# Hybrid decoder step on one core: expert queries and scores head by head, gathers behind the first query tile, and the lead of the first table at 20

## The reference

```
a  = RMSNorm(x);  p = a @ w_in            # GLA heads q,k,v,gate + MoBA heads q,k,v
o  = [gated linear attention | block attention over a paged cache]
h  = x + o @ w_out
c  = RMSNorm(h)
q  = c @ w_peer_q                         # 8 heads x 2 halves x 64
s1, s2 = q[half 0] @ sub_keys, q[half 1] @ sub_keys      # 128 keys per half
16 best of each half -> 256 sums -> 16 best: 16 experts of 16384 per token and head
g  = softmax(their scores)
hid = gelu(c . u_tab[expert]);   h += sum over heads and experts of g * hid * v_tab[expert]
h += sigmoid(h @ w_ple_gate) * (p @ w_ple_proj);  y = RMSNorm(h)
```

## Time and profile before

| | us |
|---|---|
| median of 3 runs | 2666.64 |
| profiled execution | 2673.36 |
| its span | 2671.8 |
| PE busy | 2126.1 (80%) |
| DVE busy | 1123.9 (42%) |
| POOL busy | 696.2 (26%) |
| ScalarE busy | 371.6 (14%) |

### The profile page before, as it was taken

How to read it: one execution, slowest core, us unless ns; L and a number is a source line. 1 busy time by engine, 2 the same in 40 slices (tenths; PEclk the granted TensorE clock), 3 DMA queues, 4 the chain that set the end, 5 groups by cost and what they waited for, 6 DMA issues and landing times.

```text
span 2671.8 us, 27603 instructions
## 1 busy us (share of the span) xinstructions
PE 2126.1 (80%) x9678; PEld 1228.2 (46%) x9678; DVE 1123.9 (42%) x2202; ACT 371.6 (14%) x780; POOL 696.2 (26%) x598
## 2 busy tenths in 40 slices
PE   8997899899798899467777777777777777776797
PEld 5775565555576677322222222223222222223466
DVE  2000001100185211677667667666555555445312
ACT  2000110001343000211111111111111101101111
POOL 0000000000000000464454454444444444444210
PEclk9998999999866899689999999999999998998898
DMA  4347999996421332599999999999999999999971
GB/s 158 140 163 281 364 344 367 343 355 264 168 74 45 130 141 83 229 415 422 421 421 421 422 421 421 421 421 422 421 421 422 421 421 418 421 421 421 376 287 68
DMA packets 139859, 854.80 MB, mean 320 GB/s; under 512 B 16385, under 2 KB 17218, under 8 KB 54258
## 3 DMA queue, kind: packets, MB, share of 16 engines
q0 software_dynamic: 85248, 612.41, 55.4%
q1 hardware_dynamic: 53938, 238.80, 23.5%
q10 hardware_dynamic: 576, 2.36, 0.2%
HBM read 844.07 MB, written 9.44 MB: 319 GB/s over the span
## 4 chain that ended last, share of the span: by engine, by line
DMA 43%; PE 42%; DVE 5%; issue 4%; SPq 3%; ACT 2%; POOL 1%; POOLq 0%; DVEq 0%; ACTq 0%
DMA big<-in_vt,big 32%; PE ps L736 14%; PE ps L1072 7%; PE ps L829 6%; DMA aT<-in_vt,big 5%; DMA big<-in_u,big 4%; PE ps L1097 3%; PE ps L782 2%; PE ps L845 2%; DMA subk<-in_v 1%; DVE big L1437 1%; SPq L344 1%; PE ps L1088 1%; SPq L336 1%; DMA wring<-in_u,big 1%
## 5 line engine op out<-in xcount | busy, mean ns | idle before, releaser
L1072 PE MATMUL ps<-big,wring 128*128 128x512 f32 x1232 | 583.0, 618 | 253.6 <-DMA big<-in_vt,big 206.1
L1437 DVE CUSTOM_DVE_ANT_0 big<-big 128x2048 f32<-128x2048 f32 x206 | 472.4, 2293 | 351.9 <-DMA big<-in_u,big 342.6
L1072 PEld LDWEIGHTS ps<-big,wring 128*128 128x128 f32 x1232 | 228.6, 195 | 605.9 <-issue 429.8
L1072 PE MATMUL ps<-aT,wring 128*128 128x512 f32 x816 | 375.4, 603 | 124.7 <-DMA aT<-in_vt,big 124.6
L484 POOL DMA_INDIRECT big<-in_vt,big x174 | 210.5, 1210 | 441.7 <-PE ps L1072 350.6
L476 POOL DMA_INDIRECT big<-in_u,big x206 | 238.6, 1158 | 330.3 <-DVE big L1419 254.8
L1072 PEld LDWEIGHTS ps<-aT,wring 128*128 128x128 f32 x816 | 147.7, 190 | 352.0 <-issue 228.4
L736 PE MATMUL ps<-aT,wring 128*128 128x288 f32 x1024 | 251.7, 409 | 3.2 <-DVE aT L1147 3.2
L1437 DVE CUSTOM_DVE_ANT_0 big<-wring,big 128x2048 f32<-128x2048 f32 x82 | 188.0, 2293 | 137.9 <-DMA wring<-in_u,big 134.2
L736 PEld LDWEIGHTS ps<-aT,wring 128*128 128x128 f32 x1024 | 196.2, 192 | 58.6 <-issue 4.0
L829 PE MATMUL ps<-aT,wring 128*128 128x288 f32 x768 | 207.2, 425 | 1.4 <-ACT big L543 1.4
(11 more groups left out here) (297 smaller groups left out, 1822.6 us busy)
## 6 DMA issues: line engine op xcount, KB each, us to landing
big<-in_kT SPq DMA_DIRECT2D x128, 512.0 KB, 6.2
wring<-in_w_in SPq DMA_DIRECT2D x48, 1024.0 KB, 5.1
big<-in_v SPq DMA_DIRECT2D x48, 512.0 KB, 6.5
wring<-in_v SPq DMA_DIRECT2D x32, 512.0 KB, 5.0
states<-in_v SPq DMA_DIRECT2D x32, 512.0 KB, 5.6
wring<-in_w_out SPq DMA_DIRECT2D x16, 1024.0 KB, 4.8
big<-in_w_ple SPq DMA_DIRECT2D x9, 1024.0 KB, 9.0
subk<-in_v SPq DMA_DIRECT2D x16, 512.0 KB, 6.8
```

The lines of the kernel that those rows point to most:

```text
L1072: mm = pe.matmul(ps[:, 4 * t + c, :], diag[:, j % 4, :], vring2[j % VR][:, c * 512:(c + 1) * 512], start=(j % P == 0), stop=(j % P == P - ...
L1437: dve.tensor_tensor_reduce(prod, uring[j % UR], cnat[:, tile_of(j), :], 1.0, 0.0, ALU.mult, ALU.add, hid[:, j:j + 1]).then_inc(u_read, 1)
```

## The change

1. PE works head by head: query tile 0, the scores of head 0 for both prompt groups, the transposes of prompt group 0, then query tiles 1 to 7, with the scores of head h-1 behind tile h from h = 2 on; then the scores of head 7, the transposes of group 1, and the sample scores and transposes.
2. The sample tokens are no longer repeated by DVE. PE writes them to the four quarters of the partitions, 64 matmuls of 32 columns for the scores and 64 for the transposes.
3. Query weights use two slots of `wring` only; the scores lie where the other two were. u's ring is seven slots of `big`, v's is one of `big`, two of `wring` and two of `aT`.
4. POOL issues the first u row when DVE has the first table. Its waits stand inside the loop: for the eighth query tile ahead of v 1, for the last transposes ahead of v 3.
5. LAG is 20 instead of 16.
6. ScalarE copies queries and scores head by head, with the first exponentials behind query 3 and the first GELU behind query 6. DVE waits for the scores of each next head by itself. DVE's sixteen memsets of `iota16` move ahead of the output projection.

The diff, cut to its core:

```diff
-LAG = 16
+LAG = 20
...
-        slot = [big[:, (3 + k) * D:(4 + k) * D] for k in range(8)]
-        o = 11 * D
+        slot = [big[:, 2 * D + PH * N + k * D:2 * D + PH * N + (k + 1) * D] for k in range(8)]
+        o = 10 * D + PH * N
...
-        uring = slot[0:5] + [wflat[:, (2 + k) * D:(3 + k) * D] for k in range(2)]
-        vring2 = slot[5:8] + [flata[:, k * D:(k + 1) * D] for k in range(2)]
+        scores01 = wflat[:, 2 * WS:2 * WS + 32 * P].rearrange("p (a t s k) -> p a t s k", t=2, s=2, k=P)
+        scores2 = st[:, 0:16 * P].rearrange("p (s a k) -> p s a k", s=2, k=P)
...
-            with sp.Fori(0, NPQ // SLOTS) as i:
-                weights(i, WT, A["w_pq"], W_PQ)
+            for h in range(NPQ):
+                if h < 2:
+                    sp.wait_ge(w_slots_free, NMO + NOUT + h + 1)
+                else:
+                    sp.wait_ge(query_mm, h - 1)
+                sp.dma_start(wring[:, h % 2, 0:WT], A["w_pq"][h, :, :]).then_inc(w_in[h % 2], 16)
...
-            pool.wait_ge(score_mm, 12)
-            pool.wait_ge(cn_mm, 12)
             for j in range(NU):
+                if j == 1:
+                    pool.wait_ge(query_mm, NPQ)
+                if j == 3:
+                    pool.wait_ge(cn_mm, 12)
...
+            def query_copied(h):
+                act.wait_ge(query_mm, h + 1)
+                act.activation(qpT[:, h, :], ps[:, h % 2, 0:N], ACT.Copy).then_inc(query_out, 1)
+
+            def scores_copied(h):
+                act.wait_ge(score_mm, h + 1)
+                for hf in range(2):
+                    act.activation(scores01[:, h, :, hf, :], ps[:, 2 + 2 * (h % 2) + hf, 0:2 * P].rearrange("p (t k) -> p t k", k=P),
+                                   ACT.Copy).then_inc(score_out, 1)
...
+            query_copied(0)
+            scores_copied(0)
+            turned(0)
+            for h in range(1, NPQ):
+                query_copied(h)
+                if h >= 2:
+                    scores_copied(h - 1)
+                if h == 3:
+                    exponentials(0)
+                if h == 6:
+                    gelu(0)
+            scores_copied(NPQ - 1)
+            turned(1)
+            act.wait_ge(states_gone, 1)
+            for q in range(4):
+                act.wait_ge(score_mm, PH + q + 1)
+                act.activation(scores2[:, q // 2, 4 * (q % 2):4 * (q % 2) + 4].rearrange("p a k -> p (a k)"), ps[:, q, :], ACT.Copy).then_inc(score_out, 1)
+            turned(2)
...
-                if turn_ % 2 == 0 and turn_ < 2 * heads:
+                if turn_ % 2 == 0 and 0 < turn_ < 2 * heads:
...
+            def query_tile(h):
+                pe.wait_ge(w_in[h % 2], (NMO + NOUT) // SLOTS * 16 + (h // 2 + 1) * 16)
+                if h >= 2:
+                    pe.wait_ge(query_out, h - 1)
+                for kt in range(KT):
+                    if h == 0:
+                        pe.wait_ge(normed, KT + kt + 1)
+                    mm = pe.matmul(ps[:, h % 2, 0:N], wring[:, h % 2, kt * P:(kt + 1) * P], aT[:, kt, :], start=(kt == 0), stop=(kt == KT - 1))
+                mm.then_inc(query_mm, 1)
+
+            def head_scores(h):
+                pe.wait_ge(query_out, h + 1)
+                if h == 1:
+                    pe.wait_ge(cn_out, 4)
+                if h >= 2:
+                    pe.wait_ge(score_out, 2 * h - 2)
+                for t in range(2):
+                    for hf in range(2):
+                        rows = slice(64 * hf, 64 * hf + 64)
+                        mm = pe.matmul(ps[:, 2 + 2 * (h % 2) + hf, t * P:(t + 1) * P], qpT[rows, h, t * P:(t + 1) * P],
+                                       subk[rows, h, :], start=True, stop=True)
+                mm.then_inc(score_mm, 1)
+
+            def sample_scores():
+                pe.wait_ge(score_out, 2 * PH)
...
+                        for c in range(4):
+                            mm = pe.matmul(ps[c * TS:(c + 1) * TS, q, f * P:(f + 1) * P], qpT[rows, h, T:N], subk[rows, h, :],
+                                           start=True, stop=True, tile_position=(64 * hf, c * TS), skip_group_check=True)
...
+            def turn_normed(t):
+                lo, n = TT[t]
                 for q in range(4):
-                    if t:
+                    if t == 1 and q < 2:
+                        pe.wait_ge(score_out, 2 * PH)
+                    if t == 2:
                         pe.wait_ge(cn_out, 4 * (t - 1) + q + 1)
                     for f in range(4):
                         kt = 4 * q + f
-                        src = aT[:, kt, lo:lo + n] if t < 2 else crep[:, kt, :, :].rearrange("p g n -> p (g n)")
-                        mm = pe.transpose(ps[:, 4 + q, f * P:(f + 1) * P], src, ident[:, :])
+                        if t < 2:
+                            mm = pe.transpose(ps[:, 4 + q, f * P:(f + 1) * P], aT[:, kt, lo:lo + n], ident[:, :])
+                        else:
+                            for c in range(4):
+                                mm = pe.matmul(ps[c * TS:(c + 1) * TS, 4 + q, f * P:(f + 1) * P], aT[:, kt, T:N], ident[:, :],
+                                               start=True, stop=True, tile_position=(0, c * TS), skip_group_check=True)
                     mm.then_inc(cn_mm, 1)
 
-
-
-            pe.wait_ge(score_out, 12)
+            pe.wait_ge(subk_in, 16)
+            query_tile(0)
+            head_scores(0)
+            turn_normed(0)
+            for h in range(1, NPQ):
+                query_tile(h)
+                if h >= 2:
+                    head_scores(h - 1)
+            head_scores(NPQ - 1)
+            turn_normed(1)
+            sample_scores()
+            turn_normed(2)
+            pe.wait_ge(score_out, 2 * PH + 4)
...
-            dve.wait_ge(score_out, 3)
+            dve.wait_ge(score_out, 2)
             top_head(0)
-            dve.wait_ge(normed, 2 * KT)
-            dve.wait_ge(banks_free, SLOTS + NMO + NOUT + NPQ)
-            dve.wait_ge(states_gone, 1)
-            for g in range(4):
-                dve.tensor_copy(qrep[:, :, g, :], qpT[:, :, T:N]).then_inc(rep_done, 1)
-                dve.tensor_copy(crep[:, :, g, :], aT[:, :, T:N]).then_inc(rep_done, 1)
             dve.wait_ge(cn_out, 4)
 
             for i in range(heads):
...
                 dots(j0, j0 + 4)
                 if i:
                     coefficients(2 * i - 1)
-                if i == 1:
-                    dve.wait_ge(score_out, 12)
+                if i + 1 < PH:
+                    dve.wait_ge(score_out, 2 * i + 4)
                 if i + 1 < heads:
                     top_head(i + 1)
                 weights_of(i)
                 dots(j0 + 4, j0 + 12)
                 coefficients(2 * i)
                 if 1 <= i <= PH:
+                    dve.wait_ge(score_out, 2 * PH + 4)
                     top_head(heads + i - 1)
```

More of the change, by code:

```diff
@@ L219, in program @@
         sqt = st[:, 0:N]
+        assert 2 * D + 512 <= 2 * WS
         pleT = masks[:, :, :].rearrange("p m t -> p (m t)")[:, 0:PLE // P * N].rearrange("p (k n) -> p k n", n=N)
-        pnat = [wflat[:, 0:D], st[:, 0:D]]
-        wple = ([wflat[:, D:2 * D], wflat[:, 0:D], st[:, 0:D]] + [uring[(NU - UR + i) % UR] for i in range(UR)] +
+        late0, late1 = (wflat[:, 2 * WS + k * D:2 * WS + (k + 1) * D] for k in range(2))
+        pnat = [late1, st[:, 0:D]]
+        wple = ([late0, late1, st[:, 0:D]] + [uring[(NU - UR + i) % UR] for i in range(UR)] +
                 [cnat[:, 2, :]] + [vring2[(NU - VR + i) % VR] for i in range(VR)])
@@ L617, in _, with turned @@
             root(2)
-            with act.Fori(0, NPQ // SLOTS) as i:
-                copy_out(i, W_PQ, qpT)
-            for t in range(3):
-                if t == 2:
-                    act.wait_ge(states_gone, 1)
-                for q in range(4):
-                    act.wait_ge(score_mm, 4 * t + q + 1)
-                    to, a0 = (score2, 4 * (q % 2)) if t == 2 else (score01, PH * t + 4 * (q % 2))
-                    act.activation(to[:, q // 2, a0:a0 + 4, :].rearrange("p a k -> p (a k)"), ps[:, q, :], ACT.Copy).then_inc(score_out, 1)
+            def query_copied(h):
[6 more added lines that the diff above has]
+                                   ACT.Copy).then_inc(score_out, 1)
+            def turned(t):
                 for q in range(4):
@@ L676, in _ @@
                     exponentials(heads + turn_ // 2 - 2)
-                gelu(turn_)
+                if turn_:
+                    gelu(turn_)
             diagonals(2 * P, 2 * P + 4)
@@ L1010, in _ @@
             sum_squares(1)
-            with pe.Fori(0, NPQ // SLOTS) as i:
-                tiles(i, W_PQ, aT, normed_first=KT)
-            pe.wait_ge(banks_free, SLOTS + NMO + NOUT + NPQ)
-            pe.wait_ge(roots, 2)
-            pe.wait_ge(subk_in, 16)
-            for t, (lo, n) in enumerate(TT):
-                if t == 2:
-                    pe.wait_ge(rep_done, 8)
+            def query_tile(h):
[21 more added lines that the diff above has]
```

(13 more changed lines are left out.)

23 lines of the change are left out of this document (7 added, 16 removed).

## The result

| | before | after |
|---|---|---|
| median (six runs each) | 2669.68 us | **2646.82 us** |
| all runs | 2661.25 to 2675.95 | 2642.53 to 2653.07 |
| ratio, 95% interval | | 0.9908 [0.9891, 0.9926] |
| profiled execution, span | 2671.8 | 2642.8 |

The change makes the kernel 0.9% faster, some 23 us. Predicted were 48 us and 2618 us, range 2606 to 2638: the sign is right, the size is half, and the result lies outside the range.

The account below looks back on a forecast made before the run. The DMA engines were taken to bound the kernel, full at 421 to 422 GB/s over half of the span. Start -47 and end -1 sum to -48 us, from the median 2666.6 to 2618 us; range 2606 to 2638.

Parts of the forecast that it names:

- start (first gather, weights in the way, holes): Start of the expert layer: first gather 55.8 us earlier, query weight loads +12, holes filled -3; in sum -47 us.
- v rows later by four transfers: At the end, four more u rows ahead put each v row four transfers later: +9.9 us for the first gate tile.
- lead in the steady stretch: Long stretch of expert gathers: a lead of 20 instead of 16 changes nothing, since DMA is full; 0 us.
- after row 256: Gate tiles at the end: PE's 11.2 us wait for the last u row goes, as that row is issued earlier; -11.2 us.
- +12 - 3: Start: +12 us for query weight loads now inside the gathers, -3 us for holes in DMA work that they partly fill.
- rival A: Query tiles: weight loads crowded by gathers starve PE, tile 7 ends at 1112, DMA runs dry 12 to 15 us; 2631, chance 0.12.
- rival E: Start: ScalarE's GELU between query copies holds them until 1140, so v starts no sooner; no gain, 2660 to 2670, chance 0.02.
- With a lead of 16, POOL would come to v 1 ... at a time when PE is still at tile 7: Start: reason for lead 20, with which POOL reaches v 1 after u 20, about 1091, and does not wait.
- Rival D: Long stretch: DVE's reading becomes the pace and stretches each pair; at 0.4 us a pair +54, 2721, slower; chance 0.03.
- The other wait, which I left at 7.0: End: PE's 7.0 us wait for v 267 among the gate tiles, taken to stay as it was.
- list of signs: What the trace would show: first gather near 1036, GB/s 421, no wait over 5 us before the fifth gate tile, span near 2622.
- Rival B: End: gate weights flood the queue and PE waits as long for v rows 267 to 272; +10, 2630, chance 0.13.

Follow-up runs that it names:

- e2: The kernel before with the lead of u gathers over v gathers at 20 instead of 16, nothing else: 2695.41 us, ratio 1.0091.
- e5: The kernel before with lead 20 and ScalarE's exponentials put ahead of their turn's diagonals: 2672.61 us, ratio 1.0002.
- e8: The kernel before with lead 18 and ScalarE's exponentials put ahead of their turn's diagonals: 2666.64 us, ratio 0.9984.
- e1: The changed kernel with the lead back at 16 instead of 20, all else as changed: 2621.48 us, ratio 0.9817 to the kernel before.
- e4: The changed kernel with a lead of 18 instead of 20: 2613.11 us, ratio 0.9786 to the kernel before.
- e3: The changed kernel, lead still 20, with ScalarE's exponentials ahead of their turn's diagonals instead of behind: 2621.38 us, ratio 0.9814 to the kernel before.
- e6: The changed kernel with lead 18 and exponentials ahead of the diagonals: 2610.68 us, ratio 0.9775 to the kernel before; run once more, 2614.41 us.
- e7: e6 with SP's loads of gate weights 4 to 9 also waiting for gate tile j-4: 2613.18 us, ratio 0.9777 to the kernel before.

## Why the prediction was right and wrong

The distances of the profiled executions, in us:

| kernel | tile 0 at | tile 0 to row 256 | row 256 to end |
|---|---|---|---|
| before (lead 16) | 1010.3 | 1430.4 | 231.1 |
| e2: before, 20 | 1007.2 | 1468.6 | 219.9 |
| e5: before, exponentials first, 20 | 1008.1 | 1439.8 | 221.4 |
| e8: before, exponentials first, 18 | 1015.0 | 1436.3 | 219.9 |
| **after (20)** | 1005.1 | 1415.4 | 222.4 |
| e1: after, 16 | 1013.3 | 1380.3 | 230.6 |
| e4: after, 18 | 1007.8 | 1384.4 | 220.2 |
| e3: after, exponentials first, 20 | 1009.8 | 1389.3 | 220.8 |
| e6: after, exponentials first, 18 | 1004.1 | 1384.4 | 220.1 |

(The prediction gives the end as one sum, +9.9 - 11.2; the table has its two parts apart.) The distances split the result by the prediction's own terms:

| term | forecast | measured | from |
|---|---|---|---|
| start (first gather, weights in the way, holes) | -47 | -50.1 | e1 - before |
| v rows later by four transfers | +9.9 | +9.0 | e3 - e1 |
| lead in the steady stretch | 0 | **+26.0** | after - e3 |
| after row 256 | -11.2 | -8.7 | after - before |
| sum | -48 | -23.8 | |

The spans differ by 29.0, and the other 5.2 are tile 0 that began earlier.

- **Start: right.** First gather, tile pace (8.8 to 9.7 us from one of tiles 4 to 7 to the next) and first row came as written. Of the forecast's +12 - 3 only the sum with the -55.8 can be judged; it is 3 us too cautious. One sum is off there: 1041.4 plus the 52.5 us from first dot to first row is 1093.9, not 1096; no term uses it. PE's wait of 1.6 us ahead of each of tiles 4 to 7 was 0.45 and 1.00 at two of them. A load of query weights in the crowded queue took at most 10.3 us, near the 9.8 that I read from w_pp, so rival A fell. Nothing of rival E was seen either: query copies and scores came head by head as counted.
- **"With a lead of 16, POOL would come to v 1 ... at a time when PE is still at tile 7": wrong.** In e1 POOL comes to v 1 at 1090.66, when PE has been through with tile 7 for 2.4 us, and goes on without waiting; ahead of v 3 it waits 1.51 us for the transposes, and the start keeps all its gain. The lead of 20 was not needed for it.
- **"In the steady stretch the lead changes nothing: DMA is full at either value": this is the step that failed**. The term was set to 0 and measured +26.0 us (after - e3); e2 - e5 gives 28.7 for it in the old kernel. I asked whether the queue is full and not whether every engine between u and v may run that far apart. The 17 rows of room can be counted in the code, and the trace of before shows that they were nearly used: 12.3 us of waits for the exponentials at a lead of 16, in two places.
- **Rival D had the place and not the cause.** POOL held up in `gather_u` with v behind it, DVE late: that is what it names, and its sign of being wrong appeared, slices under 415 GB/s with POOL waiting for DVE. But I priced DVE by its own work (62 us of 79.5 a head) and concluded that it has time. It has; it loses 283.8 us waiting for ScalarE, which is 14% busy. The price (0.4 us a pair) was guessed, measured are 26.0 / 256 = 0.10, below the break-even of 0.19, hence still a gain.
- **End: right in the kind, nearly in size.** The 11.19 us wait for the diagonal of the last row is gone in every kernel with a lead of 18 or 20, and is there with 16. PE in e1:

```profile
2489.34 1.94 PE L1146 MATMUL ps<-aT,wring 128*32 128x512 f32 x8 [12.26 <-ACT wring L671]
```

The last u row is read at 2486.70 now (2532.24 before). The other wait, which I left at 7.0, is 8.88 us, PE after:

```profile
2463.39 7.17 PE L1155 MATMUL ps<-xT,wring 128*128 128x256 f32 x32
...
2491.78 1.94 PE L1146 MATMUL ps<-wring 128*32 128x512 f32 x8 [8.88 <-DMA wring<-in_vt,big]
```

That is 1.9 of the 2.5 us by which the end fell short. The list of signs had promised no wait of over 5 us before the fifth gate tile, although the sum itself left 7.0 us there; the 8.88 us come ahead of the third. Rival B (nothing recovered at the end, 2630) is nearer to the measured 2647 than the forecast is, for a reason that did not occur.

- **The rest of the 28.8 us between 2618 and 2646.8** is 3.0 from the median of before (2669.68 in six runs, 2666.64 in three), and some 1.5 that is scatter.

The range was too narrow because both of its ends came from costs at the start and at the end; it had no term for the one stretch that I set to zero, half of the span.

Open remains PE's last wait. Pacing the gate weights and moving the row left it at 8.9 us; its cause is not shown, and what would shorten it wasn't found. And POOL's stands are covered at 4.3 us, dip the rate at 6.3 and 7.6 without a cost that the distances show (e4), and are not covered in the changed kernel, where they last 11.4 us and more, 13.6 in the mean (298.3 / 22); where exactly the cover ends wasn't tried.

## What to carry to other kernels

When one stream is to lead another by more, find each in-order engine that serves both and count how many rows of the follower it must have finished before it serves the leader again: here 17, on an engine that is busy 14% of the time. The cheap cure is in that engine's order: what the leading stream waits for goes ahead of what waits for the following one. Where a term is set to zero over half of the span, name what would have to be true on every engine, and look in the trace of before for a wait of the new kind that is small now; and read the GB/s line, since a digit of 9 hides a loss of 3%.

## What the runs showed of the hardware

- An indirect gather costs POOL 0.94 us to issue, and mostly 2.1 to 2.5 when a dot of DVE runs at that time (POOL's rows at 1191.26 and 1208.96 above). Between 1150 and 2400 us of the changed kernel the issues that meet no dot have a median of 0.94 us and none takes over 1.2; of some 260 that meet one, 200 take over 2. Why some of these stay short is open. In the changed kernel, where POOL catches up after each stand while DVE does the same, POOL's busy time rose from 696.2 to 851.4 us for the same 576 gathers, and in e3 it is 697.7. It did not reach the end of the kernel: a pair at 2 x 2.44 us is still under 4.97, and e4, with 768.8 us of POOL, is as fast as e6 with 686.5.
- The DMA engines keep 421 GB/s for 1200 us with one core at work, and a hole in their supply is not made up for later: no slice of any run here is above 422.
- A 1 MB load on the hardware queue that goes out singly among full gather queues lands soon: the query weights in 10.6 us at most (10.3, 10.5 and 10.6 in after, e1 and e6), the paced gate weights of e7 in 8.8 (median). In the changed kernel seven gate weights go out within 8.3 us (2460.56 to 2468.89), and the nine that go into `big` have a median of 26.5 us; in the kernel before and in e1, where the first seven of them go out 5.6 to 10.9 us apart, it is 9.0.
